# Moving the activation sums of a seven-product feed-forward from GpSimd to VectorE, and reordering ScalarE's copies at its start and end

## The reference

```python
def swiglu(x, w_gate_up, w_down):
    g, u = jnp.split(x @ w_gate_up, 2, axis=-1)
    return (jax.nn.silu(g) * u) @ w_down
h = h + rms_norm(swiglu(rms_norm(h, ffn_norm_pre), w_gate_up, w_down), ffn_norm_post)
```

## Time and profile before

| what | value |
|---|---|
| median of 3 runs | 2060.59 us (2060.29 to 2064.71) |
| the profiled execution: its own time | 2060.0 us |
| its span in the profile | 2058.2 us |
| mean granted TensorE clock | 0.994 |
| TensorE busy | 2021.8 us, 98% of the span |
| VectorE busy | 1489.6 us, 72% |
| ScalarE busy | 894.8 us, 43% |
| GpSimd busy | 104.5 us, 5% |

### The profile page before, as it was taken

The page is one execution under the profiler, slowest core; times in us unless marked ns, Lnnn a source line. Parts: engine busy times, 40 slices in busy tenths (PEclk is TensorE's granted clock), DMA queues, the critical chain, the costliest instruction groups (busy, mean ns, idle before and its releaser), DMA issues. The chain is left out here.

```text
span 2058.2 us, 31854 instructions
## 1 busy us (share of the span) xinstructions
PE 2021.8 (98%) x12178; PEld 1781.9 (87%) x12178; DVE 1489.6 (72%) x2446; ACT 894.8 (43%) x1577; POOL 104.5 (5%) x59
## 2 busy tenths in 40 slices
PE   9999999999999999999999999999999999999998
PEld 8888899988889898898887799998888777999887
DVE  6646999843784766757757999962498979999534
ACT  4224555532623323333235455542334564555323
POOL 0003200000000000000000600000000014000000
PEclk9999999999999999999999999999999999999999
DMA  5862323242225142151332222233222122223321
GB/s 186 113 114 82 133 101 115 102 143 87 77 102 144 62 123 83 62 143 62 99 107 82 82 103 102 102 124 121 102 104 82 42 103 104 102 102 110 146 91 61
DMA packets 43452, 211.37 MB, mean 103 GB/s; under 512 B 4007, under 2 KB 7112, under 8 KB 21976
## 3 DMA queue, kind: packets, MB, share of 16 engines
q1 hardware_dynamic: 29008, 181.48, 24.6%
q10 hardware_dynamic: 13416, 25.81, 4.7%
q0 software_dynamic: 928, 2.70, 2.6%
HBM read 187.43 MB, written 9.96 MB: 96 GB/s over the span
## 5 line engine op out<-in xcount | busy, mean ns | idle before, releaser
L1143 DVE TENSOR_TENSOR w_lo<-w_raw,w_hi 128x2048 fp32r<-128x2048 f32 (+1 forms) x95 | 178.0, 1884 | 236.5 <-ACT w_hi L643 236.5
L643 ACT ACTIVATE w_hi<-w_raw 128x2048 fp32r<-128x2048 f32 (+1 forms) x81 | 148.0, 1828 | 355.3 <-PE bank L1984 317.9
L1984 PE MATMUL bank<-x_hi,w_hi 128*128 128x512 f32 x704 | 283.5, 403 | 0.6 <-DVE w_lo L1143 0.6
L1984 PE MATMUL bank<-x_hi,w_lo 128*128 128x512 f32 x704 | 274.9, 390 | 0.0
L1984 PE MATMUL bank<-x_lo,w_hi 128*128 128x512 f32 x704 | 274.4, 390 | 0.0
L2106 PE MATMUL bank<-form_hi,f_hi 128*128 128x256 f32 x864 | 245.9, 285 | 13.0 <-ACT kept L771 13.0
L2106 PE MATMUL bank<-form_hi,f_lo 128*128 128x256 f32 x864 | 245.5, 284 | 0.0
L2106 PE MATMUL bank<-form_lo,f_hi 128*128 128x256 f32 x864 | 245.4, 284 | 0.0
L1984 PE MATMUL bank<-ring_hi,w_hi 128*128 128x512 f32 (+1 forms) x542 | 208.4, 385 | 2.2 <-DVE ring_lo L1416 2.2
L1984 PE MATMUL bank<-ring_hi,w_lo 128*128 128x512 f32 (+1 forms) x542 | 207.9, 384 | 0.0
L1984 PE MATMUL bank<-ring_lo,w_hi 128*128 128x512 f32 (+1 forms) x542 | 207.9, 384 | 0.0
(11 more groups left out here) (256 smaller groups left out, 4327.2 us busy)
## 6 DMA issues: line engine op xcount, KB each, us to landing
w_raw<-w_all SPq DMA_DIRECT2D x167, 1024.0 KB, 4.8
qk<-qk_next ACTq DMA_DIRECT2D x32, 384.0 KB, 10.8
h_save<-h ACTq DMA_DIRECT2D x3, 2048.0 KB, 13.5
h<-h_save ACTq DMA_DIRECT2D x3, 2048.0 KB, 8.6
w_raw<-w_all SPq DMA_DIRECT2D x6, 256.0 KB, 6.9
h<-x_t SPq DMA_DIRECT2D x3, 512.0 KB, 8.1
skew<-erow POOLq DMA_DIRECT2D x8, 192.0 KB, 8.7
out_t<-h SPq DMA_DIRECT2D x3, 512.0 KB, 3.0
```

Of the source, the lines that this page charges most:

```text
L643: ins = nc.scalar.activation(w_hi[slot(u)][:, part], w_raw[u % 2][:, part], ACT.Copy, scale=1.0 if g is None else g)
L1143: ins = v.tensor_tensor(w_lo[p][:, part], raw, hi, ALU.subtract)
L1984: ins = mm(out, b if flip else a, a if flip else b, start=start and n == 0, stop=stop and n == 2, **kw)
```

## The change

It takes the four activation sums from GpSimd and puts them on VectorE, ahead of `plain_unit(0)`; GpSimd keeps the scaling of the eight blocks. On VectorE the product of pair 0 moves behind `forms`, and `w_sums(5)` and the first split of unit 5 move ahead of `plain_unit(3)`. On ScalarE the first window is written out, with `keep(4, 1)` ahead of `summed_quarters(5)`. At the end of the 22 units `ff_round(fi, 0)` moves from `down` to a place between `keep(21, 1)` and `keep(21, 2)`.

```diff
 # GpSimd
-            def x_sums(fi, t, u0):
+            def x_scale(t):
                 for k in range(KC):
                     pool.wait_ge(h_ready, blocks_ready(t, k))
                     nc.gpsimd.tensor_scalar(x_f[:, k, :], h[:, k, :], gain(PRE_GAIN[t] + k), None,
                                             ALU.mult).then_inc(x_scaled, 1)
-                pool.wait_ge(x_scaled, KC * (fi + 1))
-                pool.wait_ge(xstat_done, t + 1)
-                ...
-                add(x_sum[0][:], a22, a21, ALU.subtract).then_inc(x_formed, 1)
-                pool.wait_ge(x_formed, 4 * fi + 1)
-                add(x_sum[1][:], x_sum[0][:], a11, ALU.add).then_inc(x_formed, 1)
-                add(x_sum[2][:], a11, a21, ALU.subtract).then_inc(x_formed, 1)
-                pool.wait_ge(x_formed, 4 * fi + 2)
-                add(x_sum[3][:], x_sum[1][:], a12, ALU.subtract).then_inc(x_formed, 1)
-                pool.wait_ge(x_formed, 4 * fi + 4)
 # ScalarE, in ffn
-                window(PLAIN)
+                first_quarter(PLAIN + 1)
+                keep(PLAIN, 0)
+                keep(PLAIN, 1)
+                summed_quarters(PLAIN + 1)
+                late_quarter(PLAIN + 1, QB22)
+                keep(PLAIN, 2)
+                late_quarter(PLAIN + 1, QT4)
+                keep(PLAIN, 3)
...
                 keep(l, 1)
                 round_parts(u0 + FC, [(slice(UNIT // 2, UNIT), None)], True)
+                ff_round(fi, 0)
                 keep(l, 2)
                 keep(l, 3)
...
             def down(fi, u0):
-                ff_round(fi, 0)
                 round_unit(u0 + 1)
 # VectorE, in ffn
-                    if l % 2:
+                    if l % 2 and product:
                         dve.wait_ge(evac, ev + l + 1)
                         order.wait()
                         product_of_pair(l // 2)
+                def x_sums():
+                    dve.wait_ge(x_scaled, KC * (fi + 1))
+                    dve.wait_ge(xstat_done, t + 1)
+                    ...
+                    v.tensor_tensor(x_sum[0][:], a22, a21, ALU.subtract).then_inc(x_formed, 1)
+                    dve.wait_ge(x_formed, 4 * fi + 1)
+                    v.tensor_tensor(x_sum[1][:], x_sum[0][:], a11, ALU.add).then_inc(x_formed, 1)
+                    v.tensor_tensor(x_sum[2][:], a11, a21, ALU.subtract).then_inc(x_formed, 1)
+                    dve.wait_ge(x_formed, 4 * fi + 2)
+                    v.tensor_tensor(x_sum[3][:], x_sum[1][:], a12, ALU.subtract).then_inc(x_formed, 1)
...
+                x_sums()
                 dve.wait_ge(xr_ready, t + 1)
                 plain_unit(0)
-                plain_unit(1)
+                plain_unit(1, False)
                 forms()
+                dve.wait_ge(evac, ev + 2)
+                order.wait()
+                product_of_pair(0)
                 plain_unit(2)
                 w_sums(PLAIN)
                 for step in range(4):
                     split_quarters(PLAIN, step)
+                w_sums(PLAIN + 1)
+                split_quarters(PLAIN + 1, 0)
                 plain_unit(3)
-                w_sums(PLAIN + 1)
-                for step in range(4):
+                for step in range(1, 4):
                     split_quarters(PLAIN + 1, step)
```

More of the change, by code:

```diff
@@ L593, in x_sums @@
                                             ALU.mult).then_inc(x_scaled, 1)
-                pool.wait_ge(x_scaled, KC * (fi + 1))
-                pool.wait_ge(xstat_done, t + 1)
-                a11, a12 = x_f[:, 0:4, HALVES[0]], x_f[:, 4:8, HALVES[0]]
-                a21, a22 = x_f[:, 0:4, HALVES[1]], x_f[:, 4:8, HALVES[1]]
-                add = nc.gpsimd.tensor_tensor
-                add(x_sum[0][:], a22, a21, ALU.subtract).then_inc(x_formed, 1)
-                pool.wait_ge(x_formed, 4 * fi + 1)
-                add(x_sum[1][:], x_sum[0][:], a11, ALU.add).then_inc(x_formed, 1)
-                add(x_sum[2][:], a11, a21, ALU.subtract).then_inc(x_formed, 1)
-                pool.wait_ge(x_formed, 4 * fi + 2)
-                add(x_sum[3][:], x_sum[1][:], a12, ALU.subtract).then_inc(x_formed, 1)
-                pool.wait_ge(x_formed, 4 * fi + 4)
[L607 to L611, removed]
+            x_scale(1)
+            x_scale(3)
             pool.wait_ge(unit_done, IN2)
@@ L617, in _ @@
                 pool.dma_start(bias2[:, n, :], flat.rearrange("(q x) -> q x", x=383)[:, 0:256]).then_inc(bias_loaded, 16)
-            sums(2, 5, FFN_C)
+            x_scale(5)
         @block.scalar
@@ L1284, in product_of_pair, with plain_unit @@
                                     work[:, 2:4, :].rearrange("p a s -> p (a s)"), ALU.mult).then_inc(ff_made, 1)
-                def plain_unit(l):
+                def plain_unit(l, product=True):
                     dve.wait_ge(unit_done, u0 + l + 1)
@@ L1297, in plain_unit @@
                         product_of_pair(l // 2)
+                def x_sums():
+                    dve.wait_ge(x_scaled, KC * (fi + 1))
+                    dve.wait_ge(xstat_done, t + 1)
+                    a11, a12 = x_f[:, 0:4, HALVES[0]], x_f[:, 4:8, HALVES[0]]
+                    a21, a22 = x_f[:, 0:4, HALVES[1]], x_f[:, 4:8, HALVES[1]]
+                    v.tensor_tensor(x_sum[0][:], a22, a21, ALU.subtract).then_inc(x_formed, 1)
[4 more added lines that the diff above has]
+                    v.tensor_tensor(x_sum[3][:], x_sum[1][:], a12, ALU.subtract).then_inc(x_formed, 1)
                 def forms():
```

## The result

The changed kernel took 2038.42 us (median of 4 executions, 2037.41 to 2041.74) beside 2060.44 us for the kernel before; the ratio is 0.9893, 95% interval 0.9874 to 0.9911. Over all the executions that the experiments added, the changed kernel has 12 with a median of 2039.4 us (2036.96 to 2042.00), and the kernel before has 49 with a median of 2059.8 us (2056.27 to 2064.71).

A forecast was written before the change was run, and what follows sets the result against it. TensorE, busy 2021.8 of 2058.2 us, was taken as the bound. 11.2 - 0.9 + 5.7 + 2.2 = 18.2 us off 2060.0 gives 2041.8; the median stands 0.6 higher, so 2042.4 us, range 2039 to 2050.

The forecast's parts named there:

- The cause, the order across two engines: At QT1 of unit 4, TensorE's 3.7 us wait was called an ordering fault between ScalarE and VectorE, not lacking throughput.
- The removal of 11.1 us in waits: At QT1 of unit 4, moving `keep(4, 1)` earlier was to remove TensorE's wait in three feed-forwards, 11.2 us in all.
- 2.2 us at `down`: At the start of each `down`, the earlier rounding was to remove TensorE's three waits for `ring_lo`, 2.2 us in all.
- VectorE's sums: The four activation sums of 1024 elements were to take 1.2 us each on VectorE, 3.31 us as the other bound.
- a VectorE as the bound: Rival, 10%: sums on VectorE take 2.2 us each, TensorE waits 12 us more at units 4 and 5; 2054.4 us.
- a slower kernel: Rival, 3%: sums on VectorE take 3.31 us each, slipping 25 us in all, clock loss stays; 2073 us.
- the clock does not come back: Rival, 10%: the drop at unit 4 comes from the whole thin stretch, not the stall; 5.7 us stay lost, 2048.1 us.
- depth-cycling: Skill section cited on TensorE's clock: kernels where frequent very short idles also made it oscillate; no size given.
- the three dependent sums of unit 5: VectorE's sums ahead of the first split of unit 5, taken as 2.6 us at 1.2 us per 1024 elements.
- the wait at unit 5: At QT1 of unit 5, part of the old wait was to return: 0.3 us per feed-forward, bounds 0 and 1.2.
- my chain: VectorE's steps followed from the four sums to `w_sum` of unit 6, to see whether TensorE's wait would come back.
- the clock's term: In five products from QT1 of unit 4, three feed-forwards lost 5.7 us to the low clock; all was to return.

The follow-up runs named there:

- experiments 4 and 5: 4: the kernel before with only `keep(4, 1)` moved ahead of `summed_quarters(5)`, 2046.01 us; 5: the changed kernel with it put back behind, 2039.36 us.
- slip: The changed kernel with two more VectorE passes of 1024 elements behind the activation sums, writing a scratch row; 2046.56 us.
- before: The kernel before, unedited, in its first profile; 2060.44 us.
- before_again: The kernel before, unedited, profiled a second time; 2064.20 us.
- ring_only: The kernel before with only the first rounding of `down` moved ahead of `keep(21, 2)`; 2056.23 us over 11 executions.
- stall_long: The changed kernel with 16 small chained ScalarE copies to a scratch place ahead of `keep(4, 1)`; 2060.70 us.
- stall_mid: The changed kernel with 12 small chained ScalarE copies to a scratch place ahead of `keep(4, 1)`; 2050.74 us.
- sums_only: The kernel before with only the activation sums moved from GpSimd to VectorE, all orders as before; 2052.48 us.

## Why the prediction missed its range

**What held.** The cause, the order across two engines, is shown from both sides (experiments 4 and 5). The removal of 11.1 us in waits and of 2.2 us at `down` is in the trace as forecast. VectorE's sums took 1218 to 1224 ns each against the 1.2 us taken. By the Trainium skill's formula for a float32 `tensor_tensor` add (VectorE: DVE Perf Modes, The TRN2 errata) I estimate (1024 + 151) / 0.96 = 1224 ns for such a pass, and the trace agrees. The median `form_lo` fell from 2221 ns to 1219 once GpSimd's sums were gone. The rivals of a VectorE as the bound and of a slower kernel had the right mechanism, as `slip` shows, and their condition, slow sums, did not occur. The rival that the clock does not come back is refuted: the three waits of 0.62 us brought no drop. One reading behind that rival was wrong. The clock fell a little before TensorE restarted only in the third feed-forward, at 1744.1 against 1745.33; in the first two it fell 1.4 and 1.0 us after the restart. The depth-cycling that the prediction cites beside that rival is told in the Trainium skill of one kernel, not of several. And the three dependent sums of unit 5 come to 2.4 us at the rate that the prediction gives for them, not 2.6; the trace after has 2.6 (1722.75 to 1725.34), so the slip did no harm.

**What was mis-sized: the wait at unit 5.** I took 0.3 us per feed-forward; it is 0.07. VectorE reached `w_sum` of unit 6 31.34 us after the start of the sums, and my chain had 31.7. That is 0.7 us in all, and by itself would not have left the range.

**What failed: the clock's term.** I priced the drops behind the three long waits, 5.7 us, and put the drops anywhere else in that execution at nothing, without a reason. The trace before had two more drops of 1.7 us, near 614 and 1618 us, which I never put into the sum, and the trace after has none. Between these two profiles the account closes: 11.1 + 2.2 + 5.7 + 2 x 1.7 = 22.4 us of the 22.6 between the spans. Without the 3.4, and with no wait at unit 5, it is my 18.2 + 0.8. So the profile on which I built stood 3.4 us above what the same kernel can do. It was not an unlucky one, though: its time is the median of the 49 executions to 0.2 us, and 14 of the 17 traces of all kernels have a drop near 610 us. The luck was on the side of the result, whose profiled execution is one of the three without, and whose four executions lay low. With all executions the changed kernel's median is 2039.4 us, which is within the range, if barely. A low end of 2039 left no room for any of this. The spread of single executions, 2056 to 2065 us before and 2037 to 2042 after, follows the mean granted clock (0.996 at 2056.4 and 0.992 at 2063.1 us before, 0.999 at 2037.0 and 0.996 at 2042.0 after), and so is mostly such drops. A range should have had 3 us on either side for them.

**What stays open.** The medians of all executions differ by 20.4 us. Waits (11.1 + 2.2 - 0.2) and drops behind the long waits (5.7, 6.5 and 4.8 us in `before`, `before_again` and `ring_only`, 5.6 on the mean) make 18.7. The other 1.7 us would be one drop fewer per execution at places that neither kernel edits. The traces of the changed kernel hold 0, 0 and 3 quanta there, those with the long waits untouched (before, before_again, ring_only) 2, 4 and 1. That is too few to say whether the rate differs or the draw did. Over all 17 traces, the six with waits of 1.8 us or more at the start of the units hold 15 quanta at other places (2.5 each), the eleven others 13 (1.2 each). That leans to a real difference, but nothing shows what would make it, and it stays open.

## What to carry to other kernels

Where two engines feed each other in written orders, follow the first unit of a pipeline by itself: the order that is right in the steady state put a copy behind a wait for the next unit's data, and one moved line gave about two thirds of the gain. Price a TensorE wait with the clock drop behind it, here 1.6 to 2.5 us on top of 3.7. And before a profile is used as a base, count the clock drops in it that no edit touches; they belong to the range and not to the base.

## What the runs showed of the hardware

How often a drop of the granted clock followed TensorE's wait at the start of the seven-product units, over the traces:

| longest wait there, us | kernels | drops behind it | lost by each in the five products after it, us |
|---|---|---|---|
| 4.3 | stall_long | 3 of 3 | 2.4, 2.4, 1.6 |
| 3.7 | before, before_again, ring_only | 9 of 9 | 1.6 to 2.5 |
| 2.5 | stall_mid | 2 of 3 | 1.6 |
| 1.8 | sums_only | 2 of 3 | 1.6 |
| 1.3 and less | the other kernels, 11 traces | 0 of 33 | |

The Trainium skill (TensorE: Matmul & The Clock Gate, HAM oscillation) warns of long idle gaps. Here waits of 1.8 and 2.5 us brought a drop in four of six cases, and the measurement decides: such waits are not safe, they are only less certain to cost than 3.7 us.

Away from the start of the units, every drop in the 17 traces stands at one of three places, and at each it comes and goes from one execution to the next (the fall behind TensorE's last matmul, in every trace, costs nothing):

| place | TensorE just before | traces with a drop |
|---|---|---|
| near 610 us | 16 matmuls of one column, 2.9 us, no wait | 14 of 17 |
| near 1120 us | a wait of 2.6 to 2.8 us for `o_t` | 5 of 17 |
| near 1615 us | 128-column transposes, waits of 0.5 and 1.24 us | 6 of 17 |

So a wait of about 2.7 us, which every trace has near 1120 us, brought a drop less often than one of 1.8 us at the start of the units (5 of 17 against 2 of 3, few cases), and the place with the most drops has no wait at all. The length of the wait is not the whole condition; what else counts, no run varied. The row behind the first place, in the kernel before, where the clock fell at 614.3:

```profile
611.45 2.92 PE L2399 MATMUL bank<-ones,r_pre 1*128 1x1 f32 x16
```
